# A fused two-block transformer kernel: token blocks placed 64 bytes past the weights, and five edits to the order of work

## The reference, cut to what matters

```
block 1:  y = hybrid_mixer(x)       projections of x, sparse attention with 16 index heads that choose
                                    the 64 best keys of a token, block attention, two gates, w_out
          x = layer_norm(ALPHA * x + y)
          x = layer_norm(ALPHA * x + cross_attention(x, mem))
          x = layer_norm(ALPHA * x + (silu(x @ w_g) * (x @ w_u)) @ w_down)     width 5632
block 2:  mod = silu(c) @ w_ada + b_ada          6 x 2048 values: shift, scale and gate, twice
          h = rms_norm(x) * (1 + scale1) + shift1
          p = h @ w_in;  mix = [fourier_mix(..), mlstm(..) * sigmoid(..)]
          x = x + gate1 * (mix @ w_out)
          h = rms_norm(x) * (1 + scale2) + shift2
          u = conv3(h @ w_up);  x = x + gate2 * ((silu(a) * v) @ w_down)       a, v = halves of u
          return rms_norm(x)
```

## Time and profile before

| what | value |
|---|---|
| median of 3 runs | 2719.18 us (2715.56 to 2719.55) |
| profiled execution | 2719.55 us, of it the span 2717.9 us |
| TensorE busy | 2607.9 us, 96% of the span, 18134 products |
| VectorE busy | 1651.0 us, 61% |
| ScalarE busy | 1254.1 us, 46% |
| chain that ended last | 93% TensorE |
| moved by DMA | 578.92 MB, mean 213 GB/s |
| granted TensorE clock | 0.983 of full speed on average |

### The profile page before, as it was taken

How to read it: one execution, slowest core, us unless ns; L and a number is a source line. 1 busy time by engine, 2 the same in 40 slices (tenths; PEclk the granted TensorE clock), 3 DMA queues, 4 the chain that set the end, 5 groups by cost and what they waited for, 6 DMA issues and landing times.

```text
span 2717.9 us, 46590 instructions
## 1 busy us (share of the span) xinstructions
PE 2607.9 (96%) x18134; PEld 2426.3 (89%) x18134; DVE 1651.0 (61%) x1911; ACT 1254.1 (46%) x1513; POOL 87.1 (3%) x141
## 2 busy tenths in 40 slices
PE   7999999999988999999999979999899999999997
PEld 7979999998878999999988868988799999998885
DVE  3546466545667777777676674554656565655555
ACT  3444455443444444444444444434455555554443
POOL 0000000000001000000000010000000000000000
PEclk9999999999989999999999989999999999999998
DMA  7444544556735888888877735434355555554552
GB/s 270 156 154 171 186 155 139 186 186 250 305 140 204 339 311 339 317 333 315 342 294 292 294 120 186 155 124 155 131 187 187 186 186 187 186 185 177 194 192 101
DMA packets 79985, 578.92 MB, mean 213 GB/s; under 512 B 8880, under 2 KB 9008, under 8 KB 9776
## 3 DMA queue, kind: packets, MB, share of 16 engines
q1 hardware_dynamic: 64208, 465.60, 46.7%
q0 software_dynamic: 14000, 101.46, 9.8%
q10 hardware_dynamic: 1712, 10.95, 1.1%
HBM read 575.87 MB, written 2.10 MB: 213 GB/s over the span
## 4 chain that ended last, share of the span: by engine, by line
PE 93%; DVE 3%; DMA 1%; issue 1%; ACT 1%; POOL 1%; DVEq 0%; ACTq 0%; POOLq 0%; SPq 0%
PE ps L1390 58%; PE ps L1427 24%; PE ps L1394 6%; DMA ada<-in_w_ada 1%; POOL small L394 1%; PE ps L1488 1%; PE ps L1627 0%; PE ps L1363 0%; DVE xlo L857 0%; DVE res L1067 0%; DMA mem_nat<-in_mem 0%; DVE xn L1096 0%; PE ps L1412 0%; DVE wlo L839 0%; PE ps L1661 0%
## 5 line engine op out<-in xcount | busy, mean ns | idle before, releaser
L839 DVE TENSOR_TENSOR wlo<-raw,whi 128x1024 fp32r<-128x1024 f32 x876 | 1058.6, 1223 | 818.7 <-ACT whi L471 814.6
L471 ACT ACTIVATE whi<-raw 128x1024 fp32r<-128x1024 f32 x876 | 916.9, 1059 | 1056.1 <-PE ps L1390 642.5
L1390 PE MATMUL ps<-xhi,whi 128*128 128x256 f32 x4240 | 1197.2, 282 | 21.6 <-DVE wlo L839 12.0
L1390 PE MATMUL ps<-xlo,whi 128*128 128x256 f32 x4240 | 1191.3, 281 | 0.0
L1390 PE MATMUL ps<-xhi,wlo 128*128 128x256 f32 x4240 | 1190.4, 281 | 0.0
L1390 PEld LDWEIGHTS ps<-xhi,whi 128*128 128x128 f32 x4240 | 802.1, 189 | 23.8 <-issue 12.1
L1390 PEld LDWEIGHTS ps<-xlo,whi 128*128 128x128 f32 x4240 | 803.7, 190 | 0.3
L1390 PEld LDWEIGHTS ps<-xhi,wlo 128*128 128x128 f32 x4240 | 803.3, 189 | 0.0
L1427 PE MATMUL ps<-whi,shi 128*128 128x512 f32 x992 | 307.3, 391 | 4.6 <-DVE slo L1033 4.6
L1427 PE MATMUL ps<-wlo,shi 128*128 128x512 f32 x992 | 306.4, 390 | 0.0
L1427 PE MATMUL ps<-whi,slo 128*128 128x512 f32 x992 | 306.1, 390 | 0.0
(11 more groups left out here) (250 smaller groups left out, 1450.7 us busy)
## 6 DMA issues: line engine op xcount, KB each, us to landing
raw<-in_stream SPq DMA_DIRECT2D x438, 1024.0 KB, 4.8
ada<-in_w_ada POOLq DMA_DIRECT2D x96, 1024.0 KB, 6.4
gamma<-in_ln_g ACTq DMA_DIRECT2D x3, 1024.0 KB, 8.2
beta<-in_ln_b ACTq DMA_DIRECT2D x3, 1024.0 KB, 11.6
mem_nat<-in_mem SPq DMA_DIRECT2D x2, 1024.0 KB, 7.5
res<-in_x SPq DMA_DIRECT2D x1, 2048.0 KB, 21.2
res<-in_x ACTq DMA_DIRECT2D x1, 2048.0 KB, 10.2
out<-xn SPq DMA_DIRECT2D x4, 512.0 KB, 2.7
```

The lines of the kernel that those rows point to most:

```text
L471: act.activation(whi[:, h % 4], raw[g % 4][:, 1024 * half:1024 * half + 1024], ACT.Copy)\
L839: dve.tensor_tensor(wlo[:, h % 4], raw[g % 4][:, 1024 * half:1024 * half + 1024], whi[:, h % 4].bitcast(F32), ALU.subtract).then_inc(lo_re ...
L1390: ins = pe.matmul(o, w[:, k, P * m:P * m + P], a[:, kt, 0:S], start=begins and n == 0 and m % 2 == 0, stop=ends and n == 2, skip_group_che ...
```

## The change

1. **Placement.** xhi, xlo, ohi, olo, ckhi, cklo start 64 bytes past the weights (xlo 320), their rows 1024 bytes apart. `shi` and `slo` keep distance 0 and no longer begin where xhi does. `hid` and `silu` begin 64 bytes lower than the pool, and new `dhi` and `dlo` at distance 0 serve as shi and slo in down1 and down2. Constants move to the end of the memory.
2. **Key selection** in steps of one, two, two, two and one rounds with a tile of `rest` between them. DMA and Silu of c_row go further up on ScalarE.
3. **Rows of w_ada.** The first two are asked for after `sig_ready` 4.
4. **No zero products.** The first tile of a wide stage writes with `start`, rows 128 to 255 (banks 4 to 7) of a half first, and waits for the reader of banks 0 and 1 or 2 and 3 only before the rows that write them. The hi and lo parts of the first turn (`first_turn`) are made before the last products before the stage are read, in out1, down1 and down2.
5. **Index heads** two at a time, before each tile.
6. **Gate rows** of the second gate stand after the first two chunks of up2, and the first pass of that loop, the last of up1's on VectorE and the four units of the gates are written out.

```diff
-STEP = 4
+SHIFT = 64
+APART = 256
+        at_shi = place[0]
+        place[0] += SHIFT
-        xhi = sb("xhi", [P, KT, S + STEP], F32R)
+        xhi = sb("xhi", [P, KT, S], F32R)
+        place[0] += APART
-        xlo = sb("xlo", [P, KT, S + STEP], F32R)
+        xlo = sb("xlo", [P, KT, S], F32R)
-        at_pool = place[0]
+        at_pool = place[0] + SHIFT + (at_shi - place[0]) % 1024
-        shi = sb("shi", [P, 4, S], F32R, at_xhi)
+        shi = sb("shi", [P, 4, S], F32R, at_shi)
-        hid = sb("hid", [P, FT, S], F32, at_pool)
+        hid = sb("hid", [P, FT, S], F32, at_pool - SHIFT)
+        dhi = sb("dhi", [P, 4, S], F32R, at_pool + 45056 - SHIFT)
+        dlo = [sb("dlo1", [P, 4, S], F32R, at_pool2 + 4096 - SHIFT), sb("dlo2", [P, 4, S], F32R, at_pool2 + 28672 + 1024 - SHIFT)]
...
-            pool.wait_ge(merged_ready, 4)
+            pool.wait_ge(sig_ready, 4)
             for n in range(2):
                 pool.dma_start(ada[n][:], w_ada[n]).then_inc(ada_landed[n], 16)
...
+            def first_turn(src, hi=shi):
+                for s in range(4):
+                    act.activation(hi[:, s], src[:, s], ACT.Copy).then_inc(shi_ready, 1)
...
+            g0 = AT["out1"]
+            act.wait_ge(merged_ready, 1)
+            first_turn(merged)
+            upper(g0 + 1)
             act.wait_ge(merged_ready, 4)
             act.dma_start(res[:], x.rearrange("(t p) d -> p t d", p=P)).then_inc(x_landed, 16)
             wide_start("out1", 0)
-            wide_turns("out1", merged, 4)
...
+            gate_rows(1)
             for s in range(4):
                 upper(AT["down2"] - 4 + s + 1)
...
+            act.wait_ge(conv_done, FC)
+            first_turn(hid, dhi)
             middle_tap(1, FC - 1)
-            gate_rows(1)
...
-            for n in range(TOPK // 8):
...
+            g0 = AT["qk"]
+            best_rounds(1)
+            rest(g0)
+            for s in range(3):
+                best_rounds(2)
+                rest(g0 + s + 1)
+            best_rounds(TOPK // 8 - 7)
...
+                    if s == 7:
+                        if unit == 3:
+                            first_turn("out1", merged)
+                        dve.wait_ge(weights_used, through(g + s))
...
-            def wide_open():
-
-                for b in range(8):
-                    pe.matmul(ps[:, b], zeros[:, 0:P], zeros[:], start=True, stop=False, skip_group_check=True)
+            def wide_tile(g, k, s, i=None, left=(shi, slo), first=False, reads_of=()):
+                hi, lo = left
                 steps = [(half, t) for half in range(2) for t in range(T)]
                 if s == 3:
                     steps.sort(key=lambda step: step[1])
+                if first:
+                    steps = [(half, t) for half in range(2) for t in reversed(range(T))]
                 pe.wait_ge(slo_ready, at(k + 1, i, 4))
-                for half, t in steps:
+                for n_step, (half, t) in enumerate(steps):
                     h = 2 * g + half
-                    if t == 0:
+                    if t == 0 or first:
                         pe.wait_ge(lo_ready, at(h + 1, i, 8))
-                    for a, w in ((shi, whi), (shi, wlo), (slo, whi)):
+                    if first and t == 0:
+                        for c in reads_of:
+                            if c % 2 == half:
+                                pe.wait_ge(pair_read[half], reads(c))
+                    for a, w in ((hi, whi), (hi, wlo), (lo, whi)):
...
+                                            w[:, h % 4, 512 * n:512 * n + 512], start=first and a is hi and w is whi, stop=False,
...
             for s in range(8):
+                pe.wait_ge(pair_read[(CH["q_idx"] + s // 4) % 2], reads(CH["q_idx"] + s // 4))
+                if s >= 2:
+                    pe.wait_ge(idx_relu, 2 * s - 2)
+                for t in range(T):
+                    for h in (2 * s, 2 * s + 1):
+                        r0 = IDX_DIM * (h % 2)
+                        ins = pe.matmul(ps[:, 4 + h % 4, S * t:S * t + S], qi[r0:r0 + IDX_DIM, s, P * t:P * t + P],
+                                        kiT[r0:r0 + IDX_DIM, :], start=True, stop=True, skip_group_check=True)
...
-            wide("down1", FC)
+            wide("down1", FC, (dhi, dlo[0]), (CH["up1"] + 2 * FC - 2, CH["up1"] + 2 * FC - 1))
...
-            with pe.Fori(0, FC) as i:
+            for q in range(2):
+                chunk(AT["up2"] + 4 * q, CH["up2"] + q, "T", fresh=5 if q == 0 else None)
+            gate_rows(1)
+            with pe.Fori(0, FC - 1) as i:
                 for q in range(2):
-                    chunk(AT["up2"] + 4 * q, CH["up2"] + q, "T", i=i, per=8, chunks=1, fresh=5 if q == 0 else None)
-            gate_rows(1)
-            for c in (CH["up2"] + 2 * FC - 2, CH["up2"] + 2 * FC - 1):
-                pe.wait_ge(pair_read[c % 2], reads(c))
+                    chunk(AT["up2"] + 8 + 4 * q, CH["up2"] + 2 + q, "T", i=i, per=8, chunks=1)
             pe.wait_ge(gate_ready, 2)
-            wide("down2", FC)
+            wide("down2", FC, (dhi, dlo[1]), (CH["up2"] + 2 * FC - 2, CH["up2"] + 2 * FC - 1))
```

More of the change, by code:

```diff
@@ L183, in two_blocks @@
         at_end = place[0]
-        assert at_end <= 229344, at_end
+        place[0] += 4096
+        ident = sb("ident", [P, P])
+        ones = sb("ones", [P, P])
+        zeros = sb("zeros", [P, 512], BF16)
+        dist = sb("dist", [P, 384])
+        causal = sb("causal", [P, 384])
+        chosen = sb("chosen", [P, 384])
+        row = sb("row", [P, LATENT + 2 * IDX_DIM])
+        mod = sb("mod", [P, ADA])
+        assert place[0] <= 229344, place[0]
         ckhi = sb("ckhi", [P, 2, S], F32R, at_pool + 8192)
@@ L654, in _ @@
             wide_start("out1", 0)
-            wide_turns("out1", merged, 4)
+            for s in range(1, 4):
+                upper(g0 + s + 1)
+            later_turns("out1", merged, 1, 3)
             squares(res, (1, 2), True)
@@ L678, in _ @@
             act.wait_ge(m_out, HEADS_MEM)
-            wide_turns("o_mem", omT, 1)
+            first_turn(omT)
+            for s in range(4):
+                upper(AT["o_mem"] + s + 1)
             squares(res, (3, 4), True)
@@ L773, in _ @@
             act.wait_ge(mix_m, 2 * LH)
-            wide_turns("out2", mixT, 4)
+            first_turn(mixT)
+            for s in range(4):
+                upper(AT["out2"] + s + 1)
+            later_turns("out2", mixT, 1, 3)
             squares(res, (10, 11), False)
@@ L960, in _ @@
             dve.wait_ge(cb_ready, 1)
-            g0 = AT["qk"]
-            with dve.Fori(0, 3) as i:
+            for s in range(3, 8):
+                rest(g0 + s + 1)
+            with dve.Fori(0, 2) as i:
                 for s in range(8):
-                    rest(g0 + s + 1, i, 8)
+                    rest(g0 + 8 + s + 1, i, 8)
             dve.wait_ge(att_free, 1)
@@ L1280, in _ @@
             dve.wait_ge(mix_f, LH)
[L1281 removed]
+            first_turn("out2", mixT)
+            rests_of_first_turn("out2")
+            later_turns("out2", mixT, 1, 3)
             dve.wait_ge(gate_ready, 1)
@@ L1331, in _ @@
                 beside(s, FC - 1)
+            first_turn("down2", hid, dhi, dlo[1])
             for s in range(4, 8):
                 beside(s, FC - 1)
[L1334 to L1343 removed]
+            rests_of_first_turn("down2")
+            later_turns("down2", hid, 1, FC - 2, None, dhi, dlo[1])
+            later_turns("down2", hid, FC - 1, 1, None, dhi, dlo[1])
             dve.wait_ge(gate_ready, 2)
@@ L1430, in wide_tile, with wide @@
+                    if n_step == 3 or (s < 3 and n_step == 1):
                         ins.then_inc(weights_used, 1)
-                    elif s == 3 and half == 1:
+                    elif s == 3 and n_step == 2:
+                        ins.then_inc(weights_used, 1)
+                    elif s == 3 and n_step == 1:
                         ins.then_inc(first_rows_done, 1)
-            def wide(name, turns):
-                wide_open()
+            def wide(name, turns, left=(shi, slo), reads_of=()):
@@ L1543, in _ @@
                     chunk(g + 6, c + 2, "T", (ohi, olo), 2, 8, i, 16, 3)
-            for c in (c0 + 10, c0 + 11):
-                pe.wait_ge(pair_read[c % 2], reads(c))
-            wide("out1", 4)
+            wide("out1", 4, reads_of=(c0 + 10, c0 + 11))
             pe.wait_ge(sq_ready, 2)
```

192 lines of the change are left out of this document (88 added, 104 removed).

## The result

The kernel after takes 2692.84 us (median of 4 runs, 2692.36 to 2693.34), beside 2717.37 us for the kernel before on the same chip (4 runs, 2715.15 to 2719.55): ratio 0.991, 95% interval 0.9899 to 0.9922. Predicted were 2638.4 us and a range that began at 2624 and ended at 2670. So the change is a gain, but the time lies 23 us above the end of the range. The whole difference is 24.5 us. All the terms without the placement were forecast at 23.8 us together; the placement, forecast at 57, gave nothing, as the first experiment shows.

A forecast was written before the change was run, and what follows sets the result against it. The prediction took TensorE as the bound almost everywhere. Terms of 57 + 3.8 + 6.5 + 5.4 + 4.2 + 3.3 + 0.6 = 80.8 us off 2719.18 gave 2638.4 us, range 2624 to 2670.

The forecast's parts named there:

- What bounds the kernel, and that position sets the pace: Whole kernel: TensorE is the bound, and a token block's byte distance from the weights sets its pace, 113.3 to 120.0 ns.
- The placement term: Token blocks 64 bytes past the weights: 13,536 products go from 117.6 to 113.3 ns, taken as -57 us.
- The rival of the high lock: Constant distance settles every product into a slow pattern, 120.0 ns if 64 acts like 96: 2728 us, chance 0.04.
- The rival that placement does nothing: The block pattern has another cause than address, so only the stalls go: 2695 us, chance 0.05.
- Another bound in up1: Rival: DMA or VectorE holds the pace in up1, losing 18 us of the gain: 2657 us, chance 0.06.
- The stationary side: Line 1394, token blocks as stationary operand, also at 64: 700 products, 3.3 us either way, taken as 0.
- Key selection: Selection rounds spread between qk tiles end TensorE's waits for wlo: -3.8 us, bounds -2 to -3.8.
- Index heads: Eight groups of paired heads save 3.2 us, or 10.1 if two heads run at once; middle taken, -6.5.
- Start of out1: Gap from the last gates product to out1's first wide one shrinks from 5.78 us: -5.4 us.
- rows of w_ada: Asking some 45 us sooner ends waits for the second row and a stretch at half clock: -4.2 us.
- Start of down1: Idle time and zero products ahead of down1's first wide product go: -3.3 us.
- Start of down2: Gate rows move into up2 and a 4.3 us wait remains, 7.9 for 8.2: taken as 0, 2 either way.

The follow-up runs named there:

- the first experiment: Kernel after with xhi and xlo laid out as before (distance 0, rows of 1040 bytes), other edits kept: 2693.36 us, ratio 0.9912.
- the experiment: Kernel after with index heads one at a time again, 16 groups of one head: 2702.93 us, ratio to before 0.9954.
- the one with 1.39 us: Kernel after with x at 112 bytes, down2's first tile reading the late half last, 32 short products ahead of out2: 2636.36 us, ratio 0.9704.
- the four steps: Kernel after with blocks 0 to 3 of xhi, xlo at 0, 16, 32, 48 bytes (xlo 256 further), others at 64 (320): 2651.18 us; also tried with products alone.

## Why the prediction was wrong, by its steps

*What bounds the kernel, and that position sets the pace.* Right: TensorE was and is the bound, and putting the token blocks at 112 bytes is worth 50 us on either kernel. The rule of the Trainium skill that I weighed here ("TensorE: Matmul & The Clock Gate", "Step-by-step: what each phase is for": two independent read ports, so the next weights take nothing from the running product) would make the place indifferent. The trace does not agree with that reading of it: the runs at 96 and 112 bytes differ by 82 us, and the products alone by 6.7 ns each. Whatever the ports are, the rule can't be used to say that placement is free.

*The placement term, -57.* This is the step that failed, in the sentence "block 4 is quick from its first product, ... and 12 in a row, whole, is the pattern that will now be repeated". I took a pace that I saw at one address for a property of the address. It was a property of the address and of the state in which the stream reached it: 113.3 ns behind blocks at 0, 16, 32 and 48, and 117.8 over all of up1 in the kernel after. So the term of 57 us came to nothing. Twelve products in a row looked steady, and they were; but steady is what each of the two states is. The rows could not show this: in before, a block at 64 always came after 0, 16, 32 and 48. I had a bound for it ("quick for another reason than its address") and gave it 0.05. Something in rows 2 could have warned me: block 7, at 112 bytes, was just as quick, and I had no reason for taking 64 over 112 but that the change did; two places out of four are quick and the two between them are at 119.2 and 120.0, so the pace does not change evenly with the place, and a value read at one place, in one order, was weak ground to build on.

*The rival of the high lock.* Mechanism right, place wrong. Products at a constant distance do settle into one pattern; at 96 it is 120.0 ns and 2725 us, slower than before, as written. At 64 they settle at 117.8, between the forecast and the rival. I had treated the two ends as the only outcomes.

*The rival that placement does nothing.* Its time, 2695, is within 3 us of the measured one, but its mechanism is not what happened: the products do depend on place. By luck the new even pace of 117.8 is close to the old mean of 117.6. Had the block pattern of before averaged 116, the change would have lost some 24 us there.

*Another bound in up1.* It did not come: 885 starts in 100 us with no stall, once the pace was there.

*The stationary side, 0.* 233.3 ns after and 231.7 before for the 512-column products of line 1453, +1.1 us over 700 of them; within its bounds.

*Key selection, -3.8.* Measured -3.3 inside qk and no idle time ahead of its first product (0.67 before). Right.

*Index heads, -6.5 between 3.2 and 10.1.* Mis-sized: 9.6 of the 10.4 in the table (64.59 us before and 54.98 after, from the last product of q_idx to the first of form T behind the heads), 10 in the experiment. The far end, 10.1, was nearly the truth. The Trainium skill, "TensorEngine Tiling (Array Packing)", "Key Properties", had it right that different tiles work in parallel, and the trace agrees, with eight records in 1.14 us. I split the difference between two mechanisms, one of which had to be wrong, so the middle of the pair could not come out.

*Start of out1 and rows of w_ada, -5.4 and -4.2.* Measured -9.8 together, of which 5.66 are the gap (5.78 to 0.12). Right; the break that I named after six products did not come.

*Start of down1, -3.3.* 3.43 to 0.12. Right.

*out2 and o_mem, -0.6.* o_mem gave 1.7, with its stretch at half clock gone; out2 lost 1.0: its start came 0.5 sooner behind the gate rows, and its products took 1.5 longer, with 3.4 us at a granted clock of 0.50 that before does not have there. Together -0.7. The sum is right by two errors, as I had priced no change of clock in either. Whether leaving the zero products out is what cost the clock at out2 stays open: two kernels without them kept it.

*Start of down2, 0 with 2 either way.* up2 and down2 together lost 2.6, just outside the 2 us that I gave them. The wait came as priced: 4.10 us of idle time behind the sixth product, where I had 4.3. I had read the wait in before as one for the side taps, which end at 2455.88; the row says that the gate row ended it, 0.27 us later, which changes the sum by no more. What was not priced is clock and pace. By an estimate from the rows, half clock until 2437.2, and before only until 2460.7 with products from 2458.53, is 1.3 us; half clock in the first 5.3 us of up2 in place of 3.3 is 1.0; and 117.8 ns in place of 117.6 over 4224 products is 0.8.

*Clock elsewhere.* 2.6 us in the first part of q_idx came from a stretch at half clock (105.5 to 112.3 before) that the kernel after does not have. No edit explains it, and I had no term for it; the kernel at 112 bytes, with the same edits, has 3.4 us of it.

Without placement the terms measured sum to 24.9 us in the table (27.5 less the 2.6 of the clock), beside 23.8, with errors of up to 3 us in both directions.

What stays open: what the two states are, and what decides between them where the order of products does not. The steady paces are 113.3 and 120.0 ns and, at 64 bytes, three products in 353.3 ns; all three are multiples of 6.67 ns (17, 18 and 53). That speaks for the weight load and the stream meeting at a fixed beat, with a phase that is kept from product to product. This is inferred from the paces and not shown, and the reason why the place modulo 32 counts is open too.

## What to carry to other kernels

A pace read from a stretch inside a mixed pattern is the pace of that pattern: before it is multiplied by 13,536 it wants a run in which nothing else precedes it, and here a program of products alone, 0.7 ms long, would have told 64 from 112 at once. When a stream is paced by placement, scan the placements and choose one that is quick from every start and after every predecessor tried, not one that was seen quick. And where a wait stays, put as much real work ahead of it as doesn't depend on it: at down2 all six kernels with 4.1 us idle had half clock behind it, and the one with 1.39 us did not.

## What the runs showed of the hardware

- A product of 256 columns with its own weight load takes 113.3 to 120.0 ns at a granted clock of 1.00 by the places of the token block and of the weights in SBUF alone (6%), with no other engine at work.
- At some places (64, 192) there are two steady paces on the same addresses, 113.3 ns (at 64 kept over 96 products alone and 192 in q_mem) and 117.8 (kept over 4224 in up1). What ran before can choose between them: the four steps led to 113.3 at 64 in both rows and in every chunk read, 24 products at any one of eight places to 117.8. It is not the only thing: q_mem had 113.3 in one kernel and 117.8 in another behind the same products. At 112 bytes, with weights at a multiple of 32, all eight starts and the four predecessors tried ended at 113.3.
- Two products of 64 rows on different halves of the rows start 5 to 7 ns apart: 1.14 us for eight instead of 1.13 for four.
- Behind the same 3.06 us of idle time ahead of out2 the granted clock fell to 0.50 in four kernels and stayed at 1.00 in two. Behind 4.1 us at down2 it fell in all six, for 3.4 or 6.8 us.
